# Expert outputs accumulated by scatter onto one copy of the token, pairs regrouped, one addition per tile

## The reference, cut to what matters

```
grp   = argmax(x @ w_grp + b_grp)                  # one of 4 groups
top2  = the two best of the 8 experts in that group
gates = softmax(top2 logits) * softmax(group logits)[grp]
x     = x + sum over the 2 chosen experts e of gates[e] * (silu(h @ Wg[e]) * (h @ Wu[e])) @ Wd[e]
```

## Time and profile before

| | us |
|---|---|
| median of 3 runs (lowest, highest) | 933.32 (931.43, 934.23) |
| the profiled execution | 932.86 |
| its span | 931.1 |
| PE busy | 867.7 (93%) |
| DVE / ACT / POOL busy | 339.0 / 213.6 / 89.5 |
| the SP queue's DMAs (q1) | 244.94 MB |
| POOL's DMAs (q0) | 30.02 MB |

### The profile page before, as it was taken

The page is one execution under the profiler, slowest core; times in us unless marked ns, Lnnn a source line. Parts: engine busy times, 40 slices in busy tenths (PEclk is TensorE's granted clock), DMA queues, the critical chain, the costliest instruction groups (busy, mean ns, idle before and its releaser), DMA issues.

```text
span 931.1 us, 14152 instructions
## 1 busy us (share of the span) xinstructions
PE 867.7 (93%) x5406; PEld 497.7 (53%) x5406; DVE 339.0 (36%) x813; ACT 213.6 (23%) x464; POOL 89.5 (10%) x106
## 2 busy tenths in 40 slices
PE   8999999999989999988878999989998999999784
PEld 5888888788833333333235555448973333333221
DVE  1522553542630111112044689973252111111105
ACT  4323233522311111111023132335121111111010
POOL 1400000000011111111100000000000111111110
PEclk9999999999989999999998999999998999999998
DMA  9962720695898999999999422034548999999995
GB/s 356 414 262 77 202 102 1 235 416 214 319 367 334 385 420 406 416 418 418 418 397 423 185 91 91 2 119 179 211 165 352 411 378 420 397 419 419 419 416 220
DMA packets 49442, 276.91 MB, mean 297 GB/s; under 512 B 11016, under 2 KB 11168, under 8 KB 20632
## 3 DMA queue, kind: packets, MB, share of 16 engines
q1 hardware_dynamic: 35472, 244.94, 65.2%
q0 software_dynamic: 13328, 30.02, 9.3%
q10 hardware_dynamic: 576, 1.05, 0.3%
HBM read 267.62 MB, written 30.61 MB: 320 GB/s over the span
## 4 chain that ended last, share of the span: by engine, by line
PE 66%; DMA 13%; SPq 10%; DVE 6%; issue 2%; ACT 2%; DVEq 0%; ACTq 0%; POOLq 0%
PE PS L680 13%; PE PS L1111 13%; SPq L448 10%; DMA slot<-in_experts 9%; PE PS L1230 9%; PE PS L1135 7%; PE PS L940 7%; DMA XGT<-rows,IDX 3%; PE PS L917 2%; PE PS L1087 2%; PE PS L1249 2%; DVE X L1595 2%; PE PS L1046 1%; PE PS L1156 1%; PE PS L1075 1%
## 5 line engine op out<-in xcount | busy, mean ns | idle before, releaser
L1111 PE MATMUL PS<-slot,XG 128*64 128x512 f32 x1024 | 232.5, 597 | 20.0 <-DMA slot<-in_experts 19.3
L1111 PEld LDWEIGHTS PS<-slot,XG 128*64 128x64 f32 x1024 | 69.5, 136 | 158.8 <-issue 134.6
L1924 DVE SCALAR_TENSOR_TENSOR hid_by_token<-PS,SC,SG 128x256 f32<-128x256 f32 x32 | 15.5, 484 | 343.9 <-ACT SG L1491 343.9
L680 PE MATMUL PS<-slot,HT 128*128 128x256 f32 x576 | 131.2, 382 | 2.1 <-ACT HT L1331 2.1
L1135 PE MATMUL PS<-slot,HID 128*64 128x512 f32 x512 | 120.2, 611 | 4.5 <-DMA slot<-in_experts 3.6
L680 PEld LDWEIGHTS PS<-slot,HT 128*128 128x128 f32 x576 | 107.1, 190 | 19.8 <-ACT HT L1331 4.0
L1230 PE MATMUL PS<-HC,slot 128*128 128x384 f32 x256 | 86.0, 491 | 1.6 <-DVE HC L2011 1.6
L1505 ACT ACTIVATE Y<-PS,SC 128x1024 f32<-128x1024 f32 x32 | 35.7, 1114 | 164.2 <-PE PS L1135 164.2
L1135 PEld LDWEIGHTS PS<-slot,HID 128*64 128x64 f32 x512 | 34.4, 141 | 65.5 <-issue 55.2
L1230 PEld LDWEIGHTS PS<-HC,slot 128*128 128x128 f32 x256 | 47.6, 190 | 40.2 <-issue 9.7
L1491 ACT ACTIVATE SG<-PS,SC 128x256 f32<-128x256 f32 x32 | 15.2, 475 | 210.8 <-PE PS L1111 210.8
(11 more groups left out here) (305 smaller groups left out, 829.4 us busy)
## 6 DMA issues: line engine op xcount, KB each, us to landing
slot<-in_experts SPq DMA_DIRECT2D x192, 1024.0 KB, 13.9
slot<-in_w_pw SPq DMA_DIRECT2D x12, 1024.0 KB, 10.5
slot<-in_w_in SPq DMA_DIRECT2D x11, 1024.0 KB, 11.9
outs<-slot POOLq DMA_DIRECT2D x12, 512.0 KB, 10.0
slot<-outs SPq DMA_DIRECT2D x6, 1024.0 KB, 7.7
slot<-in_w_out SPq DMA_DIRECT2D x4, 1024.0 KB, 7.5
rows<-X POOLq DMA_DIRECT2D x6, 512.0 KB, 8.4
KTC<-in_k_past POOLq DMA_DIRECT2D x1, 2048.0 KB, 13.8
```

Source lines behind the costliest of these rows:

```text
L680: last = mm(PS[:, in_bank(n), 0:UCOL], HT[:, k, P * t:P * (t + 1)], w[:, k, :], start=k == 0, stop=k == KD - 1)
L1111: last = mm(PS[CAP * e:CAP * (e + 1), 2 + p % 2, :], XG[:, p % 2, k, CAP * e:CAP * (e + 1)], w[:, k % 2, e, :], start=k == 0, stop=k == KD ...
```

## The change

`outs` gets one row per token. After gather(1) POOL stores X into `outs` (three stores of 512 KB), sets Y[:,1] to zero, and waits for the stores before gather(2). Every scatter adds to what the row holds (`compute_op=ALU.add`). Because an addition may not hit one row twice within a scatter, the experts are renumbered so that the two of a pair lie in different groups; the router's columns and the weights are rearranged on the host, and the DVE views in `group_chosen` and `first_max` change with them (same sizes). A scatter of the last pair is issued at the head of each window (`scatter_last`); in the first window all its indices are out of range. The zeroing of `outs` goes, and with it the choice code at L1895 and its waits. `combined` moves behind the loop; its result is no longer added onto X by itself, DVE makes X = (row read back) + PSUM once per tile of 1024. `outs_back` reads 512 KB per tile, and in layer 0 it stands before the first `w_pw1` load. PE runs down(14) before both halves of gate_up(15), `NEEDED` follows. The transposes at L1163 are regrouped around the banks that hold the combined result; their number stays 24. The diff, cut to its core:

```diff
-NEEDED += [HALF + n for n in (-6, -5, -8, -7, -4, -3, -2, -1)]
+NEEDED += [HALF + n for n in (-8, -7, -6, -5, -4, -3, -2, -1)]
...
-SENT = 16 * (NP - 1)
+SENT = 16 * NP
...
-        outs = [nc.dram_tensor(f"outs{lay}", [2 * TOK, D], F32, kind="Internal").ap() for lay in range(2)]
+        outs = [nc.dram_tensor(f"outs{lay}", [TOK, D], F32, kind="Internal").ap() for lay in range(2)]
...
-                    sp.dma_start(YB[lay][t], outs[lay].rearrange("(c t p) n -> t p c n", c=2, p=P)[t]).then_inc(
+                    sp.dma_start(YB[t], outs[lay][P * t:P * (t + 1), :]).then_inc(
...
-            sp.wait_ge(S("zeroed"), 16 * 4 * NT)
...
-                if i == 2:
+                if i == 0:
                     outs_back(0, n0)
...
-            nc.gpsimd.memset(Z, 0.0).then_inc(S("pool_set"), 1)
-            pool.wait_ge(S("pool_set"), 1)
-            for lay in range(2):
-                for t in range(2 * NT):
-                    store(outs[lay][P * t:P * (t + 1), :], Z, "zeroed")
...
             def scatter(lay, b, u, p):
 
-                if p:
-                    pool.wait_ge(S("scattered"), u * SENT + 16 * p)
+                pool.wait_ge(S("scattered"), u * SENT + 16 * (p + 1))
                 reached("y_ready", b + (p + 1))
                 pool.indirect_dma_start(outs[lay], bass.IndirectOffsetOnAxis(IDX[:, p, 0:1], 0), Y[:, p % 2, :], None,
-                                        bounds_check=2 * TOK - 1, oob_is_err=False).then_inc(S("scattered"), 16)
+                                        bounds_check=TOK - 1, oob_is_err=False, compute_op=ALU.add).then_inc(S("scattered"), 16)
+
+            def scatter_last(lay):
+
+                pool.indirect_dma_start(outs[lay], bass.IndirectOffsetOnAxis(IDX[:, NP - 1, 0:1], 0), Y[:, 1, :], None,
+                                        bounds_check=TOK - 1, oob_is_err=False, compute_op=ALU.add).then_inc(S("scattered"), 16)
...
-                if lay == 0:
-                    pool.wait_ge(S("zeroed"), 16 * 4 * NT)
                 gather(lay, b0, u0, 1)
+                for t in range(NT):
+                    pool.dma_start(outs[lay][P * t:P * (t + 1), :], X[:, t, :]).then_inc(S("outs_in"), 16)
+                nc.gpsimd.memset(Y[:, 1, :], 0.0).then_inc(S("pool_set"), 1)
+                pool.wait_ge(S("pool_set"), 2 + lay)
+                pool.wait_ge(S("outs_in"), 16 * NT * (lay + 1))
...
                         if p >= 1:
                             scatter(lay, b, u, p - 1)
+                        else:
+                            scatter_last(lay)
                         if p == NP - 1:
                             gather(lay, b, u, p + 2)
+                    reached("y_ready", b + NP)
...
-                    elif p == 0 and half == 0:
-                        pe.wait_ge(S("comb_added"), u * (2 * NT) + (lay + 1))
...
-                    if after < NT:
-                        x_transposes((after - 1,), range(6))
+                    if after == 1:
+                        x_transposes((0,), (0, 1, 6, 7))
+                    elif after == 2:
+                        x_transposes((1,), (0, 1, 6, 7))
+                        x_transposes((0, 1), (2, 3))
                     else:
-                        x_transposes((2,), range(6))
-                        x_transposes((0, 1, 2), (6, 7))
+                        x_transposes((2,), range(4))
+                        x_transposes((0, 1, 2), (4, 5))
+                        x_transposes((2,), (6, 7))
...
+                        if p == NP - 1:
+                            down(b, u, p - 1)
                         gate_up(b, u, p, 0)
                         if p == 0:
                             looked_up(b, u, 0, 0, slice(0, 4))
                             looked_up(b, u, 1, 1, slice(0, 4, 3))
-                        elif p == NP - 1:
-                            down(b, u, p - 1)
...
-                    combined(b, u)
+                combined(b0 + (n * NP + NP), u0 + (n + 1))
...
-                q.do(A(TB[:, :, :, 1], bc(C["tid"], 2, NE), ACT.Copy))
+                for kind in range(2):
+                    q.do(A(TB[:, :, :, kind], bc(C["tid"], 2, NE), ACT.Copy))
...
-                    if p >= 2:
-                        act.wait_ge(S("scattered"), u * SENT + 16 * (p - 1))
+                    if p:
+                        act.wait_ge(S("scattered"), u * SENT + 16 * p)
...
-                    q.do(V.scalar_tensor_tensor(SE[:, t, :].rearrange("p (g e) -> p g e", g=NG),
-                                                bc(FAR[:, t, :], 2, EPG), NEG,
-                                                LG[:, t, NG:NR].rearrange("p (g e) -> p g e", g=NG), ALU.add, ALU.add))
+                    q.do(V.scalar_tensor_tensor(SE[:, t, :].rearrange("p (e g) -> p e g", g=NG),
+                                                bc(FAR[:, t, :], 1, EPG), NEG,
+                                                LG[:, t, NG:NR].rearrange("p (e g) -> p e g", g=NG), ALU.add, ALU.add))
...
-                q.do(V.scalar_tensor_tensor(TB[:, :, :, 0], O2[:, :, :], float(TOK), bc(C["tid"], 2, NE), ALU.mult, ALU.add),
-                     S("code_ready"))
...
+                V.tensor_scalar(IDX[:, NP - 1, 0:1], C["eps"], 0.0, float(EMPTY), ALU.mult, ALU.add)
...
-                    dve.wait_ge(S("comb_added"), u * (2 * NT) + (lay + 1))
-                    for t in range(NT):
-                        for h in range(2):
-                            dve.wait_ge(S("comb_done"), u * (2 * NT) + (2 * t + h + 1))
-                            v = X[:, t, 512 * h:512 * (h + 1)]
-                            V.tensor_tensor(v, v, PS[:, (6, 2, 4)[t] + h, :], ALU.add).then_inc(S("comb_added"), 1)
-                dve.wait_ge(S("comb_added"), (u0 + n) * (2 * NT) + (lay + 1 + 2 * NT))
+
                 for t in range(NT):
                     dve.wait_ge(S(f"tile_moved{t}"), 16 * (lay + 2))
-                    for c in range(2):
-                        tt(X[:, t, :], X[:, t, :], YB[lay][t][:, c, :], ALU.add, S("x_done") if c else None)
+                    dve.wait_ge(S("comb_done"), 2 * NT * lay + 2 * t + 2)
+                    bank, in_halves = (6, 2, 4)[t], "p (h n) -> p h n"
+                    tt(X[:, t, :].rearrange(in_halves, h=2), YB[t].rearrange(in_halves, h=2), PS[:, bank:bank + 2, :],
+                       ALU.add, S("x_done"))
...
+def by_group(x):
+
+    return x.reshape(x.shape[:-1] + (NG, EPG)).swapaxes(-1, -2).reshape(x.shape)
```

More of the change, by code:

```diff
@@ L362, in build @@
         HS = slot[17][:, 0:KD * NS * HIST].rearrange("p (k b n) -> p k b n", k=KD, b=NS)
-        Z = slot[18][:, 0:D]
-        YB = [[slot[at + t][:, :].rearrange("p (c n) -> p c n", c=2) for t in range(NT)] for at in (6, 6)]
+        YB = [slot[6 + t][:, 0:D] for t in range(NT)]
         rc = Region(arena, limit)
@@ L950, in _ @@
             pe.wait_ge(S("kt_row"), 16)
-            pe.wait_ge(S("pool_set"), 2)
+            pe.wait_ge(S("pool_set"), 1)
             scores(0)
@@ L1065, in looked_up @@
                     if unit < 0:
-                        pe.wait_ge(S("code_ready"), lay + 1)
                         pe.wait_ge(S("tb_ready"), lay + 1)
@@ L1150, in combined @@
                 def combined(b, u):
-                    pe.wait_ge(S("y_ready"), b + NP)
-                    pe.wait_ge(S("idx_read"), u * UNITS + (lay + 1 + UNITS))
+                    pe.wait_ge(S("y_ready"), b)
+                    pe.wait_ge(S("idx_read"), u * UNITS + (lay + 1))
                     for t in range(NT):
@@ L1836, in first_max @@
                 for t in range(t0, t1):
-                    q.do(V.scalar_tensor_tensor(onehot[:, t, :].rearrange("p (g e) -> p g e", g=NG),
-                                                SE[:, t, :].rearrange("p (g e) -> p g e", g=NG), R8[:, best + t:best + t + 1],
-                                                bc(C["tie"], 1, NG), ALU.is_equal, ALU.mult))
+                    q.do(V.scalar_tensor_tensor(onehot[:, t, :].rearrange("p (e g) -> p e g", g=NG),
+                                                SE[:, t, :].rearrange("p (e g) -> p e g", g=NG), R8[:, best + t:best + t + 1],
+                                                bc(C["tie"], 2, NG), ALU.is_equal, ALU.mult))
                 q.settle()
@@ L1960, in moe @@
                 rows_out(b0, 0)
-                dve.sem_inc(S("comb_added"), 1)
+                V.tensor_scalar(IDX[:, NP - 1, 0:1], C["eps"], 0.0, float(EMPTY), ALU.mult, ALU.add)
                 index_out(u0, 1, -1, slice(1, 2), slice(0, 1))
@@ L2113, in arrange @@
     gains = np.stack([x["norm_mix"][0], x["norm_ffn"][0], x["norm_mix"][1], x["norm_ffn"][1]], 0)
-    router = np.concatenate([x["w_router_group"], x["w_router_expert"]], 2)
-    bias = np.concatenate([x["b_router_group"], x["b_router_expert"]], 1)
+    router = np.concatenate([x["w_router_group"], by_group(x["w_router_expert"])], 2)
+    bias = np.concatenate([x["b_router_group"], by_group(x["b_router_expert"])], 1)
```

(4 more changed lines are left out.)

## The result

The changed kernel takes **953.39 us** (median of 4 runs, 950.68 to 955.09) against 933.06 (4 runs) for the kernel before: ratio **1.0228** [1.0200, 1.0255], so it is slower by 20.3 us. The forecast was 936.5 with a range of 922 to 954. The sign was right, the size was not: +3.2 was the sum.

A forecast was written before the change was run, and what follows sets the result against it. PE was taken to bound the earlier part, DMA the later. Ends -13.5, copies +7.4 and additions +9.3 summed to +3.2 on the profiled 932.86, so 936.1, stated as 936.5 with a range of 922 to 954.

The forecast's parts named there:

- ends: At both layers' ends, one DVE addition per tile replaces half additions and later whole ones: 6.9 us earlier each, sum -13.5 us.
- copies: Three stores of X delay gather(2) by 4.0 us in layer 0, 3.4 in layer 1: +7.4; cheap ends 0.5, dear 14.4.
- additions: 15 accumulating scatters per layer also read `outs`, 0.47 us each, less DMA's free 2.15 and 2.65: +9.3; ends 0 and 23.4.
- (c): Rival: much slower, the chain of scatters becomes the bound above about 12.8 us each; 970 at 14 us, 940 to 955 at 10 to 12; chance 0.15.
- the gap of 279 to 285: Stretch of layer 0 with DMA at 109 GB/s, freed slots filled, PE having waited for gather(2); forecast to move back with gather(2).
- Edits at nothing: Zeroing gone, L1895 code, empty scatter, down(14) ahead of gate_up(15), regrouped pairs: 0 us in all.
- (a): Rival: slightly slower, the sum of the terms, 930 to 944 us; chance 0.38.
- (b): Rival: faster, stores in before gather(2)'s index, gather(2) at 266; 928.7 us, or 920 if added reads are free; chance 0.27.
- (d): Rival: no change, stores land between the cheap rows and the middle ones, losses and gains meet, 931 to 936 us; chance 0.20.
- the sum for the rows read back: Layer 1's end: scatter(14) lands by 910.1 at most, tile 0 is back at 915.1, wanted at 916.0; no wait counted.

The follow-up runs named there:

- ends_only: The kernel before with only one addition per tile from PSUM and regrouped transposes, the second half of `outs` neither read back nor added: 919.95 us, ratio 0.9876.
- ends_undone: The changed kernel with its copies early and the ends as before (six half-tile additions from PSUM, then two whole-tile additions onto X): 945.88 us, ratio 1.0146.
- early_copy: The changed kernel with its three stores of X into `outs` moved up, each right behind the same tile's store into `rows`: 930.75 us, ratio 0.9998.
- late_wait: The changed kernel with the wait for the three stores moved from ahead of gather(2) to behind it: 936.98 us, ratio 1.0066.
- early_plain: The changed kernel with its copies early and plain scatters in place of accumulating ones: 922.64 us, ratio 0.9919.
- after_order_back: The changed kernel with the order of loads and of PE's work at the last pairs as in the kernel before: 947.65 us, ratio 1.0153.
- order_back: The changed kernel with its copies early and the order of loads and PE's work at the last pairs as before: 925.70 us, ratio 0.9936.
- order_only: The kernel before with only the order of pairs 14 and 15 changed (down(14) ahead of gate_up(15), `NEEDED` with it): 938.18 us, ratio 1.0061.
- early_twice: The changed kernel with copies early, plain scatters and a second plain scatter of the same rows into another tensor behind each: 931.22 us, ratio 0.9999.

## Why the prediction was wrong in size

| term | forecast | measured | by |
|---|---|---|---|
| ends | -13.5 | -11.8, -15.1 | ends_only, ends_undone |
| copies | +7.4 | +22.6 | changed kernel less early_copy |
| of it the wait ahead of gather(2) | | +16.4 | changed kernel less late_wait |
| additions | +9.3 | +8.1 | early_copy less early_plain |
| order of the last pairs | 0 | +5.7, +5.1, +6.2 | after_order_back, order_back, order_only |

With the ends as ends_undone has them (the setting nearest to the change) and the order as after_order_back has it, the four make -15.1 + 22.6 + 8.1 + 5.7 = +21.3; measured are +20.3. With -11.8 and +6.2 instead they make +25.1. As the 22.6 is itself the changed kernel less early_copy, the sum tests only that the other three cancel in early_copy: -1.3, where -1.0 was measured (930.75 - 931.77).

That 953.4 lies inside the stated range is luck: the range reached that far for rival (c), which did not happen.

- **The step that failed most is "The copies".** Its mechanism was right: gather(2) behind the stores, PE waiting for it, and the gap of 279 to 285 moved back. Three sizes in it were off, and in layer 0 they make up the 6.7 us between my 270.0 and 276.70. I spaced the stores by 2.5 us, an estimate between zeroing stores with few loads beside them (1.6) and 3.4; beside the restarting loads they land 4.5 us apart (4.0 of the 6.7), and the last lands 16.2 us after its issue, near the 16.7 of the slowest zeroing store in the earlier trace rows, from which I had taken only the spacing. The first took 8.3 us where I took 6.7 (1.4, since it was issued 0.2 earlier). And I took 0.9 us from the last landing to gather(2), where 2.2 are needed (1.3). Even my dear end, 14.4, was too low. That the bytes themselves cost nothing more held as far as can be told: gather(2) came 20.4 us later in the two layers, and 22.6 were lost. An estimate from the Trainium skill's figure (DMA: Bandwidth & Descriptors, the anatomy of a DMA on POOL's path) is 5.6 us for all three, and by it the copies would have cost next to nothing; in the trace the last one alone has 16.2.
- **"Edits at nothing" failed for the order.** I looked at pair 15 only, where it does as I wrote (the 1.27 us for the hidden values, after which PE catches up). I had not seen that the list covers half a layer. The price falls due some 110 us ahead of the place that I had checked (355 against 466 in layer 0).
- **"The additions" held.** 0.47 us per scatter, less what DMA had free, gave 9.3, and 8.1 was measured. Neither end (0 and 23.4) came near. The Trainium skill, Collectives: The Full Stack, the bandwidth ceiling, says of a collective's reduction that the second source read is the cost and not the addition. early_twice agrees with it, as a second scatter that adds nothing costs the same within 3 us, but it doesn't prove it: no run here has the second read without the addition. Its "half" for full load isn't what one reads off the whole kernel, since scatters are a small part of the bytes.
- **"The ends" held.** 6.9 us in layer 0 (DVE's end 491.53 became 500.83, while the last unit of gate_up(15) came 16.2 later) and 6.9 in layer 1. The 0.3 us that I gave back in layer 0 for PE's transposes was wrong: they ran at twice the clock of before and ended another 1.3 us earlier, which the convolution's first matmuls then lost (22.57 against 20.88 us). The addition took 1.22 us for my 1.3, and no tile waited for the rows read back.
- **The rivals.** (a) had the direction and the two losses, but the time lies 9 us above its range of 930 to 944, by the copies and the order. (b) fell: gather(2) was never at 266. (c), the chain of scatters, showed only at its margin: scatter(14) waits for scatter(13) (8.16 us in layer 0; 9.8 from that one's start at 473.15 to its landing, where I had 8.6), but the rows read back came in time, so it set nothing. The time came out near where (c) had put it, for another reason. (d) fell as well; only with its copies placed early does the change tie (early_copy). In the sum for the rows read back I wrote 910.1 for the last landing; 893.63 + 8.1 + 8.1 is 909.8, which changes nothing.

## What to carry to other kernels

A wait for a large store that stands, in an engine's program, ahead of the issue of a transfer on the critical path costs the store's landing under load, not its size. Issue such a store where that wait is hidden, here behind the stores of `rows`, which took 22.6 us off; moving the wait alone took off 16.4. When a list of loads is reordered, find every place where the list is used and compare it there with the order in which slots come free. And take the slowest landing in the trace, not the median, as the price of waiting for several transfers in a row.

## What was not expected of the hardware

- Three stores of 512 KB in a row from POOL, beside weight loads, landed after 8.3 us for the first and 16.2 for the last, though each takes 0.5 us to issue; one alone needed 8.2 to 8.8.
- A scatter with addition occupies POOL for 1.59 us, a plain one for 1.01, the gather for 1.06. It hid here, since POOL has room.
- The second read of an addition doesn't show in the counted bytes (26.92 MB on POOL's queue against 26.89 with plain scatters), only in the time of its packets: 10.1% of the engines' span against 8.6%, and 10.1% with two plain scatters.
- PE's granted clock fell to 0.50 after a wait of 3.68 us as after one of 12.36: in the kernel before it is 0.50 from 275 to 281, in the changed kernel 0.50 from 284 to 290. It is back at 1.00 from 283 and from 292. So the longer wait for gather(2) made hardly more of PE's work run at the lower clock.
